# Router: the slots of the first expert group picked ahead of all other bookkeeping; a norm weight loaded in the merge; x and the first weights issued early

## The reference, cut to what matters

```python
xn = rms_norm(h, norm_mix_w[l])
mix = hybrid_mixer(xn, w_in[l], ...)          # attention and retention, w_in is 1024 x about 9700
h = h + mix
hn = rms_norm(h, norm_moe_w[l])
ffn = hierarchical_moe(hn, moe_w_group[l], moe_b_group[l], moe_w_expert[l], ..., moe_w1[l], moe_w3[l], moe_w2[l])
h = h + ffn
return rms_norm(h, norm_final_w)
```

## Time and profile before

| | us |
|---|---|
| median of 3 runs | 3436.21 |
| lowest and highest | 3434.36, 3438.23 |
| the profiled execution | 3434.14 |
| its span | 3431.3 |

### The profile page before, as it was taken

The page is one execution under the profiler, slowest core; times in us unless marked ns, Lnnn a source line. Parts: engine busy times, 40 slices in busy tenths (PEclk is TensorE's granted clock), DMA queues, the critical chain, the costliest instruction groups (busy, mean ns, idle before and its releaser), DMA issues. The chain is left out here.

```text
span 3431.3 us, 28269 instructions
## 1 busy us (share of the span) xinstructions
PE 2873.5 (84%) x11588; PEld 1555.2 (45%) x11588; DVE 653.9 (19%) x1741; ACT 462.8 (13%) x1050; POOL 257.5 (8%) x247
## 2 busy tenths in 40 slices
PE   6999999998665556565554599999999999999998
PEld 5888766544632222232222364444444655444443
DVE  1222222101310001001000323321210214221102
ACT  1222232110100000000000213110000222100000
POOL 1101023200000000000000400110000200200000
PEclk9999999999887878778787798999999998999999
DMA  6222211122579999999999521022221211222220
GB/s 198 60 68 68 63 55 43 62 86 74 198 299 428 428 428 428 428 429 428 428 428 427 181 76 62 30 77 87 89 74 55 83 38 61 66 81 86 74 74 37
DMA packets 196307, 590.79 MB, mean 172 GB/s; under 512 B 17522, under 2 KB 145650, under 8 KB 171506
## 3 DMA queue, kind: packets, MB, share of 16 engines
q1 hardware_dynamic: 188898, 572.66, 43.1%
q10 hardware_dynamic: 5120, 8.39, 0.7%
q0 software_dynamic: 2192, 8.39, 0.6%
HBM read 572.57 MB, written 16.84 MB: 172 GB/s over the span
## 5 line engine op out<-in xcount | busy, mean ns | idle before, releaser
L2388 PE MATMUL bank<-arena 128*128 128x512 f32 (+2 forms) x1472 | 607.2, 575 | 9.1 <-DVE arena L1753 9.1
L1145 PE MATMUL bank<-arena 128*32 128x512 f32 x2048 | 291.8, 732 | 352.2 <-DMA arena<-in_moe_w 351.2
L355 PE MATMUL bank<-arena 128*128 128x384 f32 x1280 | 434.2, 492 | 14.6 <-DMA arena<-in_w_in 14.6
L2388 PEld LDWEIGHTS bank<-arena 128*128 128x128 f32 x1472 | 275.2, 191 | 339.2 <-issue 328.4
L355 PEld LDWEIGHTS bank<-arena 128*128 128x128 f32 x1280 | 299.1, 239 | 120.6 <-DMA arena<-in_w_in 14.8
L1145 PEld LDWEIGHTS bank<-arena 128*32 128x32 f32 x2048 | 80.8, 131 | 562.5 <-issue 562.5
L2397 PE MATMUL bank<-arena 128*128 128x512 f32 x704 | 303.2, 592 | 0.0
L1868 PE MATMUL bank<-arena 128*128 128x512 f32 (+3 forms) x736 | 251.4, 500 | 0.0
L2397 PEld LDWEIGHTS bank<-arena 128*128 128x128 f32 x704 | 133.1, 189 | 168.4 <-issue 168.4
L1868 PEld LDWEIGHTS bank<-arena 128*128 128x128 f32 x736 | 138.6, 190 | 102.0 <-issue 70.1
L1397 DVE TENSOR_TENSOR arena<-bank,arena 64x512 f32<-64x512 f32 x32 | 33.4, 1044 | 606.0 <-ACT arena L1233 606.0
(11 more groups left out here) (309 smaller groups left out, 2383.5 us busy)
## 6 DMA issues: line engine op xcount, KB each, us to landing
arena<-in_moe_w SPq DMA_DIRECT2D x192, 2048.0 KB, 24.5
arena<-in_w_up SPq DMA_DIRECT2D x44, 1024.0 KB, 7.8
arena<-in_w_in SPq DMA_DIRECT2D x52, 512.0 KB, 6.2
arena<-in_w_down SPq DMA_DIRECT2D x10, 2048.0 KB, 7.8
arena<-in_w_in SPq DMA_DIRECT2D x12, 1024.0 KB, 5.2
y_slots<-arena ACTq DMA_DIRECT2D x64, 128.0 KB, 8.2
arena<-in_w_in SPq DMA_DIRECT2D x4, 2048.0 KB, 10.1
arena<-in_w_out SPq DMA_DIRECT2D x4, 2048.0 KB, 8.5
```

The source lines that it names most:

```text
L355: ins = pe.matmul(banks[s % 2][:, 0:CW], rows, w[:, k, :], start=(k == 0), stop=(k == KT - 1))
L1145: ins = pe.matmul(banks[pr][q:q + CAP, :], m.xt[:, k, c:c + CAP], up_view(m, slots[2 * e2 + up])[:, k, :], start=(k == 0), stop=(k == KT - 1))
L2388: ins = pe.matmul(banks[2 * (j % 2) + half][:, part], w[:, k, c0:c0 + P], m.aT[:, k, part], start=(k == 0), stop=(k == KT - 1))
```

## The change

Five edits:

1. x is loaded in four DMAs by tile, each with a semaphore of its own, at the head of the first norm's block; the block and the barrier of `load_x` are gone. ACT waits tile by tile, PE for the identity. Behind the norm's weight SP waits for all four tiles and then, still in that block, issues the decays, the tables and the first three chunks of `w_in` (`first_of_mixer`). The norm's scratch moves away from the ring.
2. `w_in` is laid out in DRAM in the order of the chunks, so that a chunk is one DMA with 12 KB (or 8 KB) in a row for each partition.
3. The second norm's weight is loaded in the merge, between the last `w_out` chunk and x, to an address (`NW_AT`) inside what becomes the eighth slot of the experts; the eighth expert load therefore waits for the end of the norm's DVE operations.
4. In the router the gates come behind the one-hot rows; the count by expert goes to bank 7 and has its own semaphore step. DVE makes the rank of each token straight out of PSUM, a first `m.yrel` from expert and rank alone (a rank of 32 or more is moved out of reach by 65536), and `m.G` from it. All else (the blocks of each expert, `ost`, `q`, the final `m.yrel`, the list of extra experts) comes after that.
5. SP goes into the loop of loads at once; the wait for `routed` and the trip of the list to DRAM and back stand behind the loads.

```diff
+def load_chunk(sp, A, m, G, c):
+    n = load_width(c)
+    at = KT * P * sum(load_width(i) for i in range(c))
+    src = A["w_in"][at:at + KT * P * n].rearrange("(p k n) -> p k n", p=P, k=KT)
+    sp.dma_start(m.ring[c % NSLOT][:, :, 0:n], src).then_inc(G[f"w_in{c % NSLOT}"], 16)
...
+def first_of_mixer(sp, A, m, G):
+    consts = A["consts"]
+    cols, _ = const_columns()
+    for t in range(T):
+        sp.wait_ge(G[f"x_in{t}"], 16)
...
+    sp_first(sp, A, m, G)
...
-            sp.dma_start(m.nw, w.partition_broadcast(P)).then_inc(G["norm_w_in"], 16)
+            if first:
+                first(sp)
+            if not weight_in:
+                sp.dma_start(m.nw, w.partition_broadcast(P)).then_inc(G["norm_w_in"], 16)
...
+                    if first:
+                        act.wait_ge(G[f"x_in{t}"], 16)
...
+            sp.dma_start(m.next_nw, A["norm_moe_w"][0].partition_broadcast(P)).then_inc(G["norm_w_in"], 16)
             sp.dma_start(m.h, A["x"][0].rearrange("(t p) n -> p t n", p=P)).then_inc(G["x_again"], 16)
...
     for at in range(WSLOT):
+        if at == WSLOT - 1:
+            sp.wait_ge(G["norm_out"], 2 * T)
         load_expert(sp, m, G, A, at, 0)
...
 def sp_moe(sp, m, G, A, eb_dram):
-    sp.wait_ge(G["routed"], 1)
-    sp.dma_start(eb_dram.rearrange("a b -> b a"), m.misc_i[0:MORE, 0:1]).then_inc(G["eb_sent"], 16)
-    sp.wait_ge(G["eb_sent"], 16)
-    sp.dma_start(m.eb_i[0:1, :], eb_dram).then_inc(G["eb_in"], 16)
...
     loads(NIT - 1, 24 - WSLOT)
+    sp.wait_ge(G["routed"], 1)
+    sp.dma_start(eb_dram.rearrange("a b -> b a"), m.misc_i[0:MORE, 0:1]).then_inc(G["eb_sent"], 16)
...
     dve.sem_inc(G["assigned"], 1)
-    dve.wait_ge(G["counted"], 1)
...
-    do(dve.tensor_copy(m.pos, pos))
-    do(dve.tensor_copy(m.e64[0], banks[5][:, 0:NE]))
-
+    dve.wait_ge(G["r_exp"], 2)
+    do(dve.tensor_reduce(gw, m.r8[1], AX.X, ALU.add))
...
+    dve.wait_ge(G["counted"], 1)
+    for k in range(2):
+        do(dve.tensor_tensor(prod, m.pick[k], pos, ALU.mult))
+        do(dve.tensor_reduce(rank[:, k, :], prod, AX.X, ALU.add))
+    do(dve.tensor_scalar(row, rank, float(CAP), 65536.0, ALU.is_ge, ALU.mult))
+    do(dve.tensor_tensor(row, row, rank, ALU.add))
+    do(dve.scalar_tensor_tensor(m.yrel, eid, float(CAP), row, ALU.mult, ALU.add))
...
+    picks(P, 0)
+    dve.tensor_tensor(m.G, m.G, m.G1, ALU.add).then_inc(G["g_ready"], 1)
+    dve.sem_inc(G["yo_ready"], 2)
+
+    dve.wait_ge(G["counted"], 2)
+    do(dve.tensor_copy(m.e64[0], banks[7][:, 0:NE]))
...
-def load_x(nc, m, G, A):
+def load_x(sp, m, G, A):
+    x = A["x"][0].rearrange("(t p) n -> p t n", p=P)
+    for t in range(T):
+        sp.dma_start(m.h[:, t, :], x[:, t, :]).then_inc(G[f"x_in{t}"], 16)
+    sp.dma_start(m.ident, A["consts"][:, 0:P]).then_inc(G["ident_in"], 16)
```

More of the change, by code:

```diff
@@ L320, in sp_mixer @@
             need(G["proj_done"], steps_of_chunk(c - NSLOT)[-1] + 1)
-        for src, n, dst in parts:
-            sp.dma_start(m.ring[c % NSLOT][:, :, dst:dst + n], w_in[:, :, src:src + n])\
-              .then_inc(G[f"w_in{c % NSLOT}"], 16)
+        load_chunk(sp, A, m, G, c)
 NSTEP = NPROJ + 2
@@ L775, in by_place, with norm_block @@
     return x.rearrange("q (k p) -> q p k", k=n)
-def norm_block(nc, m, G, banks, v, kind, dst, w, b=None, eps=EPS, nln=0, runs=False, further=None):
+def norm_block(nc, m, G, banks, v, kind, dst, w, b=None, eps=EPS, nln=0, runs=False, further=None, first=None, weight_in=False):
     n_in = G["norm_w_at"]
@@ L867, in _ @@
         def _(pe):
+            if first:
+                pe.wait_ge(G["ident_in"], 16)
             for i in range(2 * T):
@@ L881 @@
               "x_again"] + [f"merge_in{i}" for i in range(NSLOT)]
+NW_AT = 51800
 def merge_memory(m):
@@ L1118, in pe_moe @@
         for u in range(t + 1):
-            pe.matmul(banks[4][:, t * NE:(t + 1) * NE], m.ones if u < t else m.before,
-                      m.both[:, u, :], start=(u == 0), stop=(u == t))
+            ins = pe.matmul(banks[4][:, t * NE:(t + 1) * NE], m.ones if u < t else m.before,
+                            m.both[:, u, :], start=(u == 0), stop=(u == t))
+    ins.then_inc(G["counted"], 1)
     for u in range(T):
-        ins = pe.matmul(banks[5][:, 0:NE], m.ones, m.both[:, u, :], start=(u == 0), stop=(u == T - 1))
+        ins = pe.matmul(banks[7][:, 0:NE], m.ones, m.both[:, u, :], start=(u == 0), stop=(u == T - 1))
     ins.then_inc(G["counted"], 1)
@@ L2614, in program @@
         banks = [ctx.enter_context(nc.psum_tensor(f"bank{i}", [P, 512], f32)) for i in range(8)]
-        G = {n: ctx.enter_context(nc.semaphore(n)) for n in NORM_SEMS + ["x_in", "later_in", "sent", "y_zeroed"]}
+        G = {n: ctx.enter_context(nc.semaphore(n)) for n in NORM_SEMS + [f"x_in{t}" for t in range(T)] + ["ident_in", "later_in", "sent", "y_zeroed"]}
         G["norm_w_at"] = G["pool_at"] = G["dve_at"] = 0
@@ L2619, in program @@
         m = mixer_memory(arena)
-        norm_views(m, m.ring_at)
-        load_x(nc, m, G, A)
-        norm_block(nc, m, G, banks, 0, "rms", m.ns, A["norm_mix_w"][0])
+        norm_views(m, m.rqk_at)
+        norm_block(nc, m, G, banks, 0, "rms", m.ns, A["norm_mix_w"][0], first=lambda sp: load_x(sp, m, G, A),
+                   further=lambda sp: first_of_mixer(sp, A, m, G))
         by_token = nc.dram_tensor("by_token", (4, S, 4 * OW), f32, kind="Internal").ap()
@@ L2629, in program @@
         eb_dram = nc.dram_tensor("further_experts", (1, MORE), i32, kind="Internal").ap()
-        norm_block(nc, m, G, banks, 1, "rms", m.hn, A["norm_moe_w"][0], runs=True,
+        norm_block(nc, m, G, banks, 1, "rms", m.hn, A["norm_moe_w"][0], runs=True, weight_in=True,
                    further=lambda sp: loads_of_router(sp, m, G, A))
```

73 lines of the change are left out of this document (33 added, 40 removed).

## The result

The changed kernel takes 3415.49 us (median of 6 runs, 3413.72 to 3416.4), the kernel before 3436.13 in its 6. The ratio is 0.9941, interval 0.9931 to 0.9951: 20.6 us faster, where 27.9 were forecast, and 0.5 us above the forecast range of 3400 to 3415. The profiled execution took 3416.4 with a span of 3414.6, against 3434.14 and 3431.3.

A forecast was written before the change was run, and what follows sets the result against it. The prediction took PE as the bound in mixer, merge and second model, the weight stream in the experts. From 3434.14, -14.4 - 1.0 + 1.6 + 0.5 - 14.6 = -27.9 gave 3406.2 profiled, 3408 as median; range 3400 to 3415.

The forecast's parts named there:

- Bounds: Experts: weight stream sets the end, its gap of some 25 us keeps 11; mixer, merge, second model: PE busy.
- Head: Start of the mixer: PE's first product at 20.3 instead of 34.70, bounds 19.0 and 22.5; gain 14.4 us.
- Head clock: PE's first products: shorter idle time leaves less slow running at 1.2 GHz; gain 1.0 us, bounds 0 and 2.0.
- Merge: End of the merge: x queued behind the norm's weight delays DVE and PE; loss 1.6 us, bounds 1.2 and 2.2.
- Second norm: DVE starts earlier but its multiplies alternate with POOL's operations; loss 0.5 us, bounds gain 1.7 and loss 1.0.
- Router: Second expert's index to gather: 11.2 us instead of 25.79; gain 14.6, bounds 14.0 and 15.0; bookkeeping has 3.8 us cover.
- gather's clock: Gather behind the router: PE's clock after shorter idle time; no gain taken, bounds 0 and 2.8 us.
- Stream passes all on: Experts: the router's whole 14.6 us goes into the weight stream and by it into the next stage.
- list trip: SP's trip of the list, now behind the last loads: zero; if it stood alone, some 6 us.
- eighth load: SP's wait for the second norm before the eighth expert load, ending at about 910.4: zero.
- Rivals: Four other outcomes: clock 3404.5 (0.15), late first chunk 3412 (0.11), DVE bookkeeping 3416 (0.08), slower stream 3448 (0.04).
- The clock rival: Head and gather: PE keeps its upper clock level, another 1.0 + 2.8 us gained, 3404.5; chance 0.15.

The follow-up runs named there:

- strips_again: The changed kernel with w_in in its natural layout again, each chunk three DMAs of 512 B rows; 3422.44 us.
- no_reload: The changed kernel without the second load of x in the merge; 3400.23 us.
- best_filler5: The changed kernel without x's second load, PE's second-norm pauses filled by unread products (nine ahead, five behind each tile, three behind the last); 3393.33 us.
- norm_weight_back: The changed kernel with the second norm's weight loaded in that norm's own block again, not in the merge; 3406.56 us.
- list_trip_first: The changed kernel with SP again waiting for `routed` and sending the list to DRAM and back before its loop of loads; 3415.75 us.
- head_only: The kernel before with only x in four parts, tables and first chunks issued in the first norm's block, and w_in laid out by chunk; 3421.68 us.
- roots_first: The changed kernel, but in the second norm DVE waits for all four inverse roots before its first multiply; 3409.33 us.
- filler: The changed kernel with unread PE products in the second norm, nine ahead of the transposes, three behind each of the first three tiles; 3411.96 us.
- router_only: The kernel before with only the router's new order and SP's new order (list trip behind the loads); 3419.92 us.

## Why the prediction was right or wrong

- **Bounds.** Right in the main. The 3.49 us by which the second expert's index came earlier and the 14.63 of the router both appear at the next stage (18.39 with 0.26 more). The stream followed its restart one for one, and its hole was not used up. Its size was misjudged: 11 us were forecast to be left (9 by the prediction's own 955.0 and 946) and 18 were. The first eight loads of experts are issued with the norm, 12.63 us earlier (892.03 for 904.66), while the long logits let the router's work start only 3.49 earlier.
- **Head.** Forecast 20.3, found 20.86, inside the bounds. x landed 0.8 later than taken (SP goes on at 9.01 for 8.24), the rest was 0.2 shorter. That the norm is ready in time held, though the next block began at 19.06 and not by 18.3. My argument on edit 2 was incomplete: I gave it the difference between 5.43 and 3.9 us of landing. strips_again shows a second effect that I had no row for, SP's issue time of the strips, which would have held up the barrier. It was avoided by the change, so no error came of it.
- **Head clock.** 0.60 of 1.0, inside the bounds, but by luck: in the profiled executions of other kernels with the same head the first step took 10.67 (no_reload) to 13.69 us (best_filler5), start to start, against 12.76 in the kernel before. One trace of each can't show a gain here.
- **Merge.** x cost 1.70 of 1.6. Not forecast is the 1.68 in the output products. Nothing ties it to the change: strips_again, which has edit 3, took 14.10, and norm_weight_back, which hasn't, 15.78; see below.
- **Second norm.** On DVE's side the mechanism was right (multiplies apart, 9.56 us from first start to last end for 9.67, DVE's end 0.48 later for 0.5), and so was the rule on the shared ports. Two details were off and cancelled: a multiply took 2.0 and not 1.87, the wait behind it 0.33 to 0.60 and not 0.7. The prediction stopped at DVE's end. **This is the step that failed:** "Loss 0.5" is what the edit costs DVE; PE behind it pays 0.82 more in the last tile's transposes and 6.56 in the logits, terms that the sum put at nothing without a reason. The runs show 8.2 to 8.9 us for edit 3 where 2.1 were forecast, and best_filler5 that PE's pauses make the difference. The bounds, a gain of 1.7 and a loss of 1.0, held nothing of it.
- **Router.** 14.63 for 14.6. The counting took 4.53 as before, the gather started 11.16 after the index for 11.2, and DVE's bookkeeping did not overrun its cover. No gain from the gather's clock in this execution, as taken (10.01 for 10.17), but that too is luck: in the ten other profiled kernels with this router order the gather took 8.84 to 9.89, against 9.53 to 10.17 in the three with the old one.
- **Stream passes all on, list trip, eighth load.** Zero each; list_trip_first confirms the second.
- **Rivals.** None of the four came true. The clock rival looked at the right resource but only at the two places where idle time shrinks and only for a gain. What was missing was the question in the other direction: where does PE, now fed in portions, have new pauses? Rows of the kernel before would have warned me. Its logits at 7.34 us stand right behind transposes with a pause of 0.16, and the granted clock rises among the last of these:

```profile
904.46 5.35 PE L874 MATMUL bank<-arena 128*128 128x128 f32 x24 [6.64 <-DVE arena L849]
...
909.00:910.00 1.00, 0.84 (x7) 0.60 (x5) 0.92 (x1) 0.71 (x2) 0.00 (x0) 0.81 0.96 410
```

Seen in medians, 20.6 were gained and 27.9 forecast, 7.3 less. The 7.4 us behind the second norm are of that size; the head and its clock fell short by another 1.0, so 1 us is left that the runs' spread doesn't let one place. The profiled pair shows less, 16.7 in the span, because of two restarts of PE that go one way or the other from execution to execution (3.4 us together), and went badly in the one and well in the other.

## What to carry to other kernels

An edit that lets an engine start earlier but in portions is to be followed to the engine behind it: read whether its products come in one piece and at which granted clock, and price the products after it at both levels. Here a load moved so that DVE starts 1.6 us sooner in its block brought a loss of 8, and leaving it where DVE has to wait for it was better. When a DMA issue is moved ahead of a barrier, what counts is the time that the queue needs to issue it (17.34 us in short rows or 1.64 in long ones for the same bytes), not only the landing.

## What the runs showed of the hardware

The level of PE's clock after one and the same pause differs. In the second model PE waits 3.01 us for DVE and then does 32 products. In the kernel before:

```profile
2966.16 10.56 PE L2388 MATMUL bank<-arena 128*128 128x384 f32 x32 [3.01 <-DVE arena L1753]
```

In the changed kernel, at the same place:

```profile
2947.76 12.25 PE L2430 MATMUL bank<-arena 128*128 128x384 f32 x32 [3.01 <-DVE arena L1795]
```

In the 14 profiled executions it took 10.56 in four (before, head_only, roots_first, filler) and 12.25 in ten, in no relation to the edits. Likewise the first output products of the merge behind 2.2 us of idle: 14.10 in before, head_only, router_only and strips_again, 15.68 to 15.78 in the others that reload x. In the changed kernel the trace shows the clock falling to 0.50 from 816 to 819 and back at 1.00 from 820; in the kernel before it stayed at 1.00. What decides stays open. It puts 1.7 us of noise on a comparison of two executions at each such place.

DVE's multiply takes 1.87 us in a row of four and 1.99 to 2.04 apart. A row of products of 72 columns can lose the level that it began with (11.91 us in roots_first) and hold it in another run (7.34 in best_filler5). PE had pauses ahead of it in the first and hardly any in the second, but as the level's changes also fall by chance, where the line runs was not measured.
